# S5 branch: real and imaginary parts side by side in the free axis, its tables made one block ahead, and another order ahead of it

## The reference

```
h = RMSNorm(x) * (1 + scale1) + shift1        # scale, shift from silu(c) @ w_mod + b_mod
P = h @ W_in                                   # columns for Hyena, GLA, S5 and the gates
S5, per direction (f, b) and group g of 32, state p of 64, complex:
  lam_dt = lam * exp(log_dt);  b_bar = (exp(lam_dt) - 1) / lam * (b_re + i b_im)
  x_t = exp(lam_dt) x_{t-1} + b_bar u_t        # u_t: 16 inputs of the group
  y_t = Re(c_mat x_t)                          # both directions summed
y_s5 = gelu(y + d*u) * sigmoid(gelu(..) @ w_glu + b_glu)
mix = W_out( sum_b sigmoid(g_b) * (y_b @ W_b) );  x += gate1 * mix
x += gate2 * SwiGLU(RMSNorm(x) * (1 + scale2) + shift2)
```

## Time and profile before

| | |
|---|---|
| runs | 1380.88, 1381.2, 1385.95 us |
| the profiled execution | 1383.87 us, of which its span 1382.0 us |
| TensorE busy | 1191.1 us (86%) |
| VectorE, ScalarE, GpSimd busy | 550.8, 415.6, 401.6 us |
| mean granted TensorE clock | 0.923 |

### The profile page before, as it was taken

One profiled execution on the slowest core, in us unless ns is written; L12 is line 12 of the kernel. 1 busy time (PEld: TensorE's weight loads), 2 busy tenths in 40 slices (PEclk: granted clock), 3 DMA queues, 4 the chain that ended last, 5 costly groups with the idle time before them and its releaser, 6 DMA issues.

```text
span 1382.0 us, 15272 instructions
## 1 busy us (share of the span) xinstructions
PE 1191.1 (86%) x5933; PEld 906.6 (66%) x5933; DVE 550.8 (40%) x998; ACT 415.6 (30%) x758; POOL 401.6 (29%) x341
## 2 busy tenths in 40 slices
PE   4699799787688888888959899979989999999996
PEld 1278658675466667667746355639878888888884
DVE  3764435643665455445630557353420001200013
ACT  2653214413343433333404111003422321232321
POOL 2033014402103113112203110113255554556541
PEclk9899889888898989889969999999999999999998
DMA  9711131933121211222215130574423323333211
GB/s 329 229 62 46 33 120 55 193 123 92 31 77 39 76 54 55 53 69 84 66 41 183 45 107 31 197 229 137 123 61 92 94 102 95 92 99 113 86 54 61
DMA packets 139987, 135.68 MB, mean 98 GB/s; under 512 B 13209, under 2 KB 126041, under 8 KB 138892
## 3 DMA queue, kind: packets, MB, share of 16 engines
q1 hardware_dynamic: 126432, 105.58, 26.3%
q0 software_dynamic: 4384, 17.50, 3.7%
q10 hardware_dynamic: 9100, 11.64, 2.7%
HBM read 121.59 MB, written 11.01 MB: 96 GB/s over the span
## 4 chain that ended last, share of the span: by engine, by line
PE 53%; DVE 15%; ACT 5%; issue 3%; POOL 1%; DMA 1%; DVEq 0%; ACTq 0%; POOLq 0%
PE psum L681 45%; PE psum L900 2%; PE psum L930 1%; PE psum L933 1%; PE psum L931 1%; ACT L1459 1%; DVE buf L2055 1%; DVE buf L1994 1%; DVE buf L1996 1%; POOL ring_lo L1221 1%; DVE buf L1995 1%; DVE buf L1973 1%; DVE buf L1974 1%; DMA buf<-in_w_out 1%; DVE buf L1978 1%
## 5 line engine op out<-in xcount | busy, mean ns | idle before, releaser
L1221 POOL TENSOR_TENSOR ring_lo<-buf,ring_hi 128x512 fp32r<-128x512 f32 (+1 forms) x260 | 339.1, 1337 | 760.1 <-ACT ring_hi L1378 760.0
L681 PE MATMUL psum<-hT_hi,ring_hi 128*128 128x512 f32 x712 | 292.8, 411 | 22.3 <-ACT buf L1539 6.1
L681 PE MATMUL psum<-hT_lo,ring_hi 128*128 128x512 f32 x712 | 284.9, 400 | 0.0
L681 PE MATMUL psum<-hT_hi,ring_lo 128*128 128x512 f32 x712 | 284.3, 399 | 0.0
L1378 ACT ACTIVATE ring_hi<-buf 128x512 fp32r<-128x512 f32 (+1 forms) x260 | 139.6, 610 | 237.2 <-PE psum L681 160.9
L681 PE MATMUL psum<-buf,buf 128*128 128x512 f32 (+1 forms) x448 | 190.7, 583 | 10.0 <-DVE buf L2074 5.0
L681 PEld LDWEIGHTS psum<-hT_hi,ring_hi 128*128 128x128 f32 x712 | 139.1, 195 | 55.2 <-issue 16.3
L681 PEld LDWEIGHTS psum<-hT_lo,ring_hi 128*128 128x128 f32 x712 | 138.8, 195 | 30.3 <-issue 1.9
L681 PEld LDWEIGHTS psum<-hT_hi,ring_lo 128*128 128x128 f32 x712 | 138.4, 194 | 30.2
L681 PEld LDWEIGHTS psum<-buf,buf 128*128 128x128 f32 x448 | 87.8, 198 | 103.8 <-issue 90.3
L2266 DVE TENSOR_TENSOR buf<-psum,buf 128x512 f32<-128x512 f32 x22 | 15.2, 692 | 220.8 <-PE psum L681 220.8
(11 more groups left out here) (331 smaller groups left out, 1774.3 us busy)
## 6 DMA issues: line engine op xcount, KB each, us to landing
buf<-in_w_in SPq DMA_DIRECT2D x26, 1024.0 KB, 5.3
buf<-in_w_mod SPq DMA_DIRECT2D x24, 1024.0 KB, 7.7
buf<-in_w_ffn_in SPq DMA_DIRECT2D x44, 512.0 KB, 5.1
buf<-in_w_ffn_out SPq DMA_DIRECT2D x8, 1024.0 KB, 5.0
scr_k<-buf POOLq DMA_DIRECT2D x4, 1024.0 KB, 5.5
buf<-scr_k POOLq DMA_DIRECT2D x4, 1024.0 KB, 7.6
buf<-in_w_out SPq DMA_DIRECT2D x4, 1024.0 KB, 6.3
buf<-in_w_ffn_out SPq DMA_DIRECT2D x4, 768.0 KB, 4.4
```

The lines of the kernel that those rows point to most:

```text
L681: ins = nc.tensor.matmul(o, a, b, start=start and n == 0, stop=stop and n == len(pairs) - 1)
L1221: nc.gpsimd.tensor_tensor(ring_lo[:, a:a + n], ring[:, a:a + n], ring_hi[:, h + i * n:h + i * n + n].bitcast(fp32), SUB)\
```

## The change

The change has two parts.

**S5.** Two groups now share the 128 partitions (64 states each), and the real and imaginary parts stand side by side in the free axis (index ri; q counts pairs of groups). A swap of the parts is then only another read order. So Wsw, sw, the swap matrix, and `s5_z` go. Tables per group (angles, powers, factors, B and C matrices) have half the columns. V9 and Mt have two buffers each. `s5_v`, `s5_k` and the Toeplitz copy of a round are made two rounds before its scan's result is used; `s5_k`'s evacuation is a step of its own, `s5_ka`. `s5_d` writes 64 output partitions at a time, `s5_k` and `s5_y` contract 64 partitions at a time in most products.

**Ahead of S5.** The A1 factors and the normalisation of x come before the filter norm; the squares for a filter norm are a step `fsq` of their own, ahead; the second filter norm stands behind the q projection; the `a` projection comes before the second filter spectrum; the modulation transposes stand some steps behind their products; `s5_turn`, `s5_angles` and `s5_factors` stand in the GLA part; modulation blocks 18 and 19 stand before the last GLA steps.

The core of the diff:

```diff
@@ buffers
-        V9 = {d: r.take(GB * 9 * 16)... for d in FB}
-        Mt = v3(r.take(GB * P), GB)
+        V9 = {d: [r.take(576).rearrange("p (r q t j) -> p r q t j", r=2, q=2, t=9) for _ in range(2)] for d in FB}
+        Mt = [v3(r.take(GB * P), GB) for _ in range(2)]
@@ order ahead of S5
+        step("A1")
+        step("xn")
         step("fnorm", 0)
-        step("xn")
         step("hT")
...
-        step("fnorm", 1)
         cols_slot("q", Q0)
         step("chan", "q", ("q0", "q1"), False)
+        step("fsq", 1)
+        step("fnorm", 1)
         step("q_ev")
-        step("fspec", 1, 0)
-        step("fspec", 1, 1)
         cols_slot("a", A0, 128)
         step("chan", "a", ("a",), True)
         step("a_ev")
+        step("fspec", 1, 0)
+        step("fspec", 1, 1)
         step("z")
...
-        mod_steps(12, 17)
+        mods(12, 17)
         step("gla_exp", 1)
+        step("s5_turn")
+        step("s5_angles")
         cols_slot("r1", R0 + 256)
         step("rhalf", 1)
+        mods_T(12, 17)
         step("gla_states", 1)
+        step("s5_factors")
         step("gla_att", 0)
-        mod_steps(13, 15)
+        mods(13, 15)
         for b in range(1, 4):
             step("gla_att", b)
             step("gla_out", b - 1)
+            if b == 1:
+                mods_T(13, 15)
+                mods(14, 16)
             if b == 2:
-                mod_steps(14, 16)
+                mods_T(14, 16)
+                mods(18, 19)
@@ the S5 loop
         for m in range(2 * NB):
             step("s5_r", b, n)
+            if m + 1 < 2 * NB:
+                step("s5_ka", *divmod(m + 1, 2))
             one_beside()
             if m + 1 < 2 * NB:
                 step("s5_d", *divmod(m + 1, 2))
-            step("s5_z", b, n)
+            step("s5_x", b, n)
+            if m + 2 < 2 * NB:
+                step("s5_gen", *divmod(m + 2, 2))
             if n == 0 and b:
                 step("s5_y", b - 1)
-            step("s5_x", b, n)
-            step("s5_v", b, n)
             if m + 2 < 2 * NB:
-                step("s5_gen", *divmod(m + 2, 2))
+                step("s5_v", *divmod(m + 2, 2))
             one_beside()
-            step("s5_k", b, n)
             if m + 2 < 2 * NB:
                 step("s5_w", *divmod(m + 2, 2))
+                step("s5_k", *divmod(m + 2, 2))
@@ TensorE
             def s5_d(b, n):
...
+                for q in range(2):
+                    for ri in range(2):
+                        for h in range(2):
+                            s = slice(64 * h, 64 * h + 64)
+                            ins = nc.tensor.matmul(o[s, ri, q, :], Wt[:, ri, q, s], U[:, GB * b + 2 * q + h, :],
+                                                   start=True, stop=True)
             def s5_k(b, n):
...
+                for q in range(2):
+                    for ri in range(2):
+                        for h in range(2):
+                            s = slice(64 * h, 64 * h + 64)
+                            ins = nc.tensor.matmul(banks[h][0:16, q * P:(q + 1) * P], Bb[d][1 + ri][s, 2 * b + q, :],
+                                                   V9[d][b % 2][s, ri, q, n:n + 8, :]..., start=ri == 0, stop=ri == 1)
             def s5_y(b):
...
+                for q in range(2):
+                    for h in range(2):
+                        nc.tensor.matmul(oo, Mt[b % 2][:, 2 * q + h, :], U[:, GB * b + 2 * q + h, NSC:NS], ...)
+                        for n, d in enumerate(FB):
+                            for ri in range(2):
+                                w = V9[d][b % 2][s, ri, q, 1 - n:9 - n, :]...
+                                ins = nc.tensor.matmul(oo, w, Xc[d][b % 2][s, ri, q, :], ...)
@@ ScalarE
             def s5_w(b, n):
-                A(Wt, o, ACT.Copy)
-                A(Wsw[:, :, 0:64], o[:, :, 64:P], ACT.Copy)
-                A(Wsw[:, :, 64:P], o[:, :, 0:64], ACT.Copy, scale=-1.0)...
+                A(Wt.rearrange("p r q n -> p (r q n)"), o, ACT.Copy).then_inc(freed(name), 1)
@@ VectorE
             def s5_v(b, n):
-                if b:
-                    full(dve, f"y5{b - 1}")
-                dve.wait_ge(S("Xc"), 2 * b + n + 1)
+                if b > 1:
+                    both(dve, full, f"y5{b - 2}")
...
+                for ri in range(2):
+                    go(V.tensor_tensor(vv_[:, ri, :, :, :], power(Lr, t_, n, b, ri, shape), cs[0], MUL))
+                    go(V.tensor_tensor(vtmp[:, ri, :, :, :], power(Li, t_, n, b, ri, shape), cs[1], MUL))
             def s5_ka(b, n):
...
+                for h in range(2):
+                    k7 = Kall[0:16, h::2, 7, :]
+                        go(V.tensor_tensor(k7, o[:, :, 0, :], v3(dtmp, GB)[:, h::2, :], ADD))
             def s5_x(b, n):
+                go(V.tensor_tensor(zi, turned(c[:, :, lat]), Zs[:, :, :, lat], MUL))
+                link(V.tensor_tensor(zt, s[:, :, :, lat], Zs[:, ::-1, :, lat], MUL))
```

More of the change, by code:

```diff
@@ L36, in constants @@
     ident = np.eye(P, dtype=f32)
-    swap = np.zeros((P, P), f32)
-    for m in range(64):
-        swap[m + 64, m] = 1.0
-        swap[m, m + 64] = -1.0
     s = np.arange(P)[:, None]
@@ L505, in hybrid_block @@
         step("s5_w", 0, 1)
+        step("s5_v", 0, 1)
+        step("s5_k", 0, 0)
+        step("s5_ka", 0, 0)
+        step("s5_k", 0, 1)
         for m in range(2 * NB):
@@ L612, in hybrid_block @@
                  for x in ([("split", n) for n in ahead.get(at, [])] + [st])]
-        k_at = {st[1]: at for at, st in enumerate(UNSPLIT) if st[0] == "s5_k" and st[2] == 1}
+        k_at = {st[1]: at for at, st in enumerate(UNSPLIT) if st[0] == "s5_ka" and st[2] == 1}
         mt_before = {}
@@ L633, in freed, with both @@
             return bank_free[jobs[name][0]]
+        def both(eng, wait, name):
+            for h in range(2):
+                wait(eng, f"{name}{h}")
         def evacuated(eng, name):
@@ L935, in s5_y @@
-                close(ins, name)
+                pe.wait_ge(S(f"Mt{b % 2}"), 16 * 8 * (b // 2 + 1))
+                banks = [open_job(f"y5{b}{h}") for h in range(2)]
+                for q in range(2):
+                    for h in range(2):
+                        s = slice(64 * h, 64 * h + 64)
+                        oo = banks[h][:, q * NSL:(q + 1) * NSL]
+                        nc.tensor.matmul(oo, Mt[b % 2][:, 2 * q + h, :], U[:, GB * b + 2 * q + h, NSC:NS],
+                                         start=True, stop=False)
+                        for n, d in enumerate(FB):
+                            for ri in range(2):
+                                w = V9[d][b % 2][s, ri, q, 1 - n:9 - n, :].rearrange("p t j -> p (t j)")
+                                ins = nc.tensor.matmul(oo, w, Xc[d][b % 2][s, ri, q, :], start=False,
+                                                       stop=n == 1 and ri == 1)
+                        if q:
+                            close(ins, f"y5{b}{h}")
@@ L1129, in _ @@
                           gla_states=gla_states, gla_att=gla_att, gla_out=gla_out, gla_T=gla_T, rhalf=rhalf, s5_init=s5_init,
-                          s5_w=s5_w, s5_d=s5_d, s5_k=s5_k, s5_z=s5_z, s5_y=s5_y,
+                          s5_w=s5_w, s5_d=s5_d, s5_k=s5_k, s5_y=s5_y,
                           glu=glu, merge_g=merge_g, merge_b=merge_b,
@@ L1250, in hy_tok @@
             def hy_tok():
-                full(pool, f"y5{NB - 1}")
-                pool.wait_ge(S("s5_end"), 1)
+                both(pool, full, f"y5{NB - 1}")
                 pool.wait_ge(S("Yd"), 16 * 16)
@@ L1489, in s5_y @@
             def s5_y(b):
-                name = f"y5{b}"
-                o = full(act, name)
                 if b == NB // 2:
@@ L1506, in s5_gelu @@
                 act.wait_ge(S("Yd"), 16 * 16)
-                full(act, f"y5{NB - 1}")
+                both(act, full, f"y5{NB - 1}")
                 full(act, f"b1{KD - 1}")
@@ L1549, in hy_tok @@
             def hy_tok():
-                act.wait_ge(S("s5_end"), 1)
-                full(act, f"y5{NB - 1}")
+                both(act, full, f"y5{NB - 1}")
                 act.wait_ge(S("Yd"), 16 * 16)
@@ L1739, in a_ev @@
             def a_ev():
-                full(dve, "H111")
-                dve.wait_ge(S("spill"), 64)
                 for tag, c, N in (("C", 0, LC), ("L", LC, L)):
@@ L1753, in z @@
             def z():
+                full(dve, "H111")
+                dve.wait_ge(S("spill"), 64)
                 for n, d in enumerate(FB):
@@ L1950, in powers @@
-            def powers(span, gs, shape):
-                return (x[:, span, gs].rearrange("p t g -> p g t").unsqueeze(3).to_broadcast(shape) for x in (Lr, Li))
+                Cr, Cn, Cx = Cm
+                for k, dst in enumerate((Cr, Cn)):
+                    name = f"s5c{k}"
+                    o = full(dve, name).rearrange("p (q h i) -> p q h i", h=2, i=16)
+                    for h in range(2):
+                        s = slice(64 * h, 64 * h + 64)
```

(14 more changed lines are left out.)

358 lines of the change are left out of this document (160 added, 198 removed).

## The result

The changed kernel takes 1303.1 us (median of 4 runs, 1301.13 to 1304.51) where the kernel before took 1382.6 in the same series: ratio 0.942, interval [0.940, 0.945]. The profiled execution took 1303.52 us, its span 1301.7. The forecast was 1289, its own range 1262 to 1312.

A forecast was written before the change was run, and what follows sets the result against it. TensorE was taken as the bound, near its limit behind S5, losing time to waits and slow clock in the loop. -44 - 13 - 13 - 11 - 11 = -92 us from 1383.87 gave execution 1292, predicted time 1289; own range 1262 to 1312.

The forecast's parts named there:

- loop: S5 loop, first unit to end of last: 310 us falls to 266, as Toeplitz waits and most half-speed time go; -44 us.
- end of the loop: From the last unit to the next stage: 10 to 12 us instead of 24.4; -13 us (bounds -7 and -17).
- S5's set-up: Angles and factors move into the GLA part, removing 13.2 us of TensorE's wait; -13 us (bounds -5 and -18).
- GLA part: Later modulation transposes and earlier blocks 18 and 19 save 14.3 us, less 3 for VectorE; -11 us (bounds 0 and -15).
- front: Ahead of GLA: -4 from normalising x first, -7 from earlier a copy and z products; -11 us (bounds 0 and -18).
- TensorE's own work: In the S5 loop, 232 us at full clock after the change against 230 before, so it does not shrink.
- lower bound of 2.7: s5_y, per block: 5.1 us forecast, but 2.7 if the halves ran beside each other; upper bound 8.5 at half clock.
- new waits: In the S5 loop, VectorE leading in some rounds and ScalarE's cosines holding a copy: 20 us allowed (bounds 5 and 60).
- half clock behind waits: In the S5 loop, half-speed time after the new waits: 14 us allowed (bounds 0 and 35).
- The fall follows the waits: S5 loop: TensorE's clock drops after waits; after one of 3.10 us a branch unit takes 5.62 instead of 3.59 us.
- VectorE did not bound the loop: Denies the rival that VectorE or ScalarE bounds the S5 loop, about 18.5 us a round, total 1330 us; chance 0.24.
- Rival 3: VectorE's new read orders are slow, 2.6 times the cost, 24.4 us a round in the loop; total 1402 us; chance 0.07.

The follow-up runs named there:

- the Toeplitz part one block later: The changed kernel with V9, K and the Toeplitz copy of a round made in the round itself, behind x: 1379.6 us, ratio 0.998.
- the kernel with late factors: The changed kernel with the 16 small VectorE operations of the S5 factors moved behind the last GLA output: 1307.4 us, ratio 0.944.
- the kernel with the old front: The changed kernel with filter norm before normalised x and A1 factors, second norm before q, second spectrum before a, as before the change: 1303.8 us, ratio 0.943.
- the alternating kernel: The changed kernel with each pair's full-height products in s5_y first, then the eight half-height ones, lower and upper half by turns: 1279.2 us, ratio 0.924.

## Why the prediction was right, and where it was not

The total lies 14 us above the forecast and in its own range. That it came so near is in part luck: S5's loop gained 8 us more than forecast, while some 18 of the 22 us expected ahead of S5's set-up did not come. The terms:

| term | forecast | measured |
|---|---|---|
| loop | -44 | -52.3 |
| end of the loop | -13 | -10.3 |
| S5's set-up | -13 | -11.7 (57.9 to 46.2 us) |
| GLA part | -11 | -5 |
| front | -11 | 0, or +1.5 |
| behind S5 | 0 | -2.4 |

The GLA part is counted from its first chain of states to the gates (87.9 to 82.8 us), the front up to that chain (248.5 to 250.1), which scatters by 3 us between kernels with the same list.

*TensorE's own work*, forecast 232 us at full clock: 258.0 less 1.3 of waits, less 28 for 22% of the time at half clock, is 229. Inside it `s5_d` (0.88 for 1.1) and `s5_k` (1.05 for 1.25) are cheaper and `s5_y` (5.6 for 5.1) is dearer. Its lower bound of 2.7, "if the halves ran beside each other", was almost within reach: 3.2 in another order. I had priced the order as written and not asked whether it had to be written so. The split of the 5.1 us was off too. A pair of groups takes 2 x 1.40 = 2.80 us with four changes of height and, with the same products in turn, 2.12 with two; if nothing else differs, a change costs 0.34 us and not 0.1 (an estimate), and the products themselves less than the 0.11 us an instruction that I took.

*Waits and clock.* The 30 us of waits for DMAs and WT went as forecast. I allowed 20 us for new waits, and there were 1.3. I allowed 14 us for half clock behind waits; it was 28, behind none. This is the step that failed: "The fall follows the waits". It does where there are waits (the Toeplitz part one block later shows it at 0.80), but the one-sided order of `s5_y` lowers the clock by itself. The two errors offset each other, -19 and +14, and the rest is the 3 us of own work.

*The end and the set-up* were right in kind and nearly in size. The wait of 7.57 us became one of 4.0 for VectorE's `s5_x`, and `s5_y` runs at half clock there, 10 us; the 13.2 us for ScalarE went, and 4.4 us for the second WT came.

*GLA part.* I allowed 3 us for the angles and factors on VectorE. They cost 6.4 less 2.7, as the kernel with late factors shows: the 16 small operations stand between the chain of states and the first mask, which the trace of before would have let me place. Not seen at all was the copy of block 15, which waits 4.81 us for the transpose of block 13 because both use the row buffer of odd blocks, and the transposes now come later. The wait that I had called only replaced, for the split ahead of the r1 projection, is 9.4 us where 7.9 stood.

*Front.* The filter norm still ended at the same time. I had not followed ScalarE's queue: the squares for the norm now stand ahead of its square root for rms, so VectorE's reciprocal starts at 55.82 instead of 51.57 us, and modulation rows, A1 and transposes with it. With the squares behind, it starts at 50.41, and the gates behind GLA 4.9 us earlier, at 328.0. But the kernel with the old front has them at 328.1. So moving the squares cost what it gives back here, and the rest of the new front gains nothing: the 11 us were not there to be had.

*Rivals.* VectorE did not bound the loop of the changed kernel, although its busy time came out above the forecast (196.5 us, 13.1 a round, for 11.6). It begins to once `s5_y` is short: in the alternating kernel TensorE waits 10.2 us for V9. Rival 3 was not only unlikely but its row was misread. I took the mean of 752 ns of L2055 for the price of a reversed write. In the trace of before that line takes 0.42 us in the first round and 1.31 in the second, and a split lies beside the second:

```profile
415.84 5.20 POOL L1221 TENSOR_TENSOR ring_lo<-buf,ring_hi 128x512 fp32r<-128x512 f32 x4 [42.70 <-ACT ring_hi L1378]
418.05 0.42 DVE L2050 TENSOR_TENSOR buf<-buf,psum 128x256 f32<-128x256 f32 x1 [2.99 <-PE psum L920]
418.57 1.31 DVE L2055 TENSOR_TENSOR buf<-buf,buf 128x256 f32<-128x256 f32 x1
434.61 5.36 POOL L1221 TENSOR_TENSOR ring_lo<-buf,ring_hi 128x512 fp32r<-128x512 f32 x4 [13.57 <-ACT ring_hi L1378]
436.66 0.97 DVE L2055 TENSOR_TENSOR buf<-buf,buf 128x256 f32<-128x256 f32 x1
506.12 0.43 DVE L2055 TENSOR_TENSOR buf<-buf,buf 128x256 f32<-128x256 f32 x1
```

The second round is also one that writes reversed, so its rows alone leave it open. The third and the sixth close it: the third writes forward, beside a split, and takes 0.97 us; the sixth writes reversed, with no split beside it, and takes 0.43. Without GpSimd's subtraction the same operation has a mean of 425 ns over all 16 rounds, reversed or not (L2084 above). The mean of 752 mixed the prices with and without a split, and the trace of before could have told. L2050, which reads one operand from PSUM, keeps its 0.42 us beside the split. The overlap is also why VectorE's 11.6 us a round became 13.1: `s5_x` and `s5_gen` now follow each other with SBUF operands alone, where the split falls, and without the subtraction the loop's VectorE work is 40 us less.

*The signs it named.* A round took 17.2 us, `s5_d` 0.88, and no wait for a DMA was left, as said. The clock of the loop was 0.89 and not 0.93, VectorE's busy time 13.1 us a round and not below 12.5, and the gates behind GLA began 3.5 us earlier and the loop 15.3, not 20 and 35. Two groups of `s5_x` had means of 962 and 903 ns, above double the 420 of the earlier trace rows, which the prediction had named as a sign of being wrong; it was the overlap with the split.

## What to carry to other kernels

Products on half the height belong together, alternating between the halves, with the full-height ones ahead of them: 3.2 instead of 5.6 us a block, and the clock stays up where no wait stands ahead. A wait of a few us ahead of a run of small products costs twice, once itself and once by the clock behind it, so making the data a block earlier was worth 70 to 76 us where those waits summed to 42 and all idle time to 61. Where a group's mean lies far above a single instance, look at what the other engines do beside the long ones before giving it a cause; and where an edit ahead shows its gain in the trace but not in the time, look at the clock behind it.

## What the hardware showed that I had not expected

TensorE's clock fell to half in a stretch with no idle time at all, in products of 64 rows and columns on one half after another (0.95, then 0.50, in neighbouring 4 us), and stayed up in the same products alternated (all seven blocks of the loop at 1.11 us for 16 instructions), unless a wait of some 5 us stood ahead (1.97). VectorE's operations on SBUF operands took 1.5 us instead of 0.42 beside GpSimd's subtraction; a TENSOR_SCALAR with a single SBUF operand was slowed too (1.32 us instead of 0.25), an operation with a PSUM operand was not, and GpSimd's own time stayed between 5.0 and 5.6 us. When GpSimd only wrote (530 ns per memset), VectorE was not slowed (420 and 425 ns).
